# Decoder layer with attention, SSD and PEER: other instruction orders around the first gathers, part of a convolution on GpSimd, other places for late query weights

## What is computed

```python
proj = x @ w_in                      # x: 256 tokens x 1024
attn = dsa_attention(q, k, v, iq, ik, iw)   # indexer picks 64 keys for each query
ssd  = ssd_mixer(z, xbc, dt)         # depthwise conv of 4 taps, SiLU, scan in 2 chunks, gated norm
h    = LayerNorm(alpha * x + concat(attn, ssd) @ w_out)
# PEER, for each of 8 heads: scores against 2 x 128 keys, the 16 best pairs choose
# 16 of 16384 experts for each token
act  = gelu(h . u[expert]) * gate    # u, v: rows of 1024
out  = LayerNorm(alpha * h + sum over 8 x 16 experts of act * v[expert])
```

## Time and profile before

| | us |
|---|---|
| median of 3 runs | 869.95 |
| lowest, highest | 869.11, 871.92 |
| the profiled execution, its own time | 869.6 |
| its span, first to last instruction | 867.9 |
| PE, DVE, ACT, POOL busy | 574.1, 548.5, 449.4, 283.7 |

### The profile page before, as it was taken

One profiled execution on the slowest core, in us unless ns is written; L12 is line 12 of the kernel. 1 busy time (PEld: TensorE's weight loads), 2 busy tenths in 40 slices (PEclk: granted clock), 3 DMA queues, 4 the chain that ended last, 5 costly groups with the idle time before them and its releaser, 6 DMA issues.

```text
span 867.9 us, 10158 instructions
## 1 busy us (share of the span) xinstructions
PE 574.1 (66%) x3343; PEld 477.7 (55%) x3343; DVE 548.5 (63%) x1398; ACT 449.4 (52%) x804; POOL 283.7 (33%) x267
## 2 busy tenths in 40 slices
PE   7979897879576667777666554450754646555576
PEld 4458567566475666666555454350653645555532
DVE  3466556558706475656858676739968585857455
ACT  1125103645435544864867566553965665756432
POOL 0000000415224233454662544430753435344400
PEclk9979998989786789898996877865868768677689
DMA  8981003759978989999999999999999999999993
GB/s 302 386 310 50 0 1 98 266 223 399 420 268 337 407 311 392 359 404 414 421 423 420 422 420 422 420 423 422 389 421 423 423 420 422 423 422 421 422 421 132
DMA packets 58521, 301.08 MB, mean 347 GB/s; under 512 B 5576, under 2 KB 16112, under 8 KB 25712
## 3 DMA queue, kind: packets, MB, share of 16 engines
q0 software_dynamic: 36864, 268.45, 75.5%
q1 hardware_dynamic: 20400, 31.92, 10.4%
q10 hardware_dynamic: 1216, 0.19, 0.1%
HBM read 299.49 MB, written 1.05 MB: 346 GB/s over the span
## 4 chain that ended last, share of the span: by engine, by line
PE 39%; DMA 33%; DVE 13%; ACT 10%; issue 4%; POOL 1%; DVEq 0%; SPq 0%; ACTq 0%; POOLq 0%
DMA arena<-in_expert_uv,expert 29%; PE bank L620 11%; PE bank L601 7%; PE bank L470 7%; DVE arena L1439 4%; PE bank L585 3%; PE bank L482 3%; ACT arena L982 3%; PE bank L640 3%; DMA mix<-in_peer_wq 3%; ACT weight L972 2%; POOL arena L441 1%; PE bank L460 1%; DMA arena<-in_w_idx 1%; PE bank L610 1%
## 5 line engine op out<-in xcount | busy, mean ns | idle before, releaser
L620 PE MATMUL bank<-ident,arena 128*128 128x128 f32 x1920 | 307.4, 332 | 247.5 <-ACT arena L982 247.5
L441 POOL DMA_INDIRECT arena<-in_expert_uv,expert x256 | 282.0, 1102 | 542.0 <-PE bank L620 293.9
L620 PEld LDWEIGHTS bank<-ident,arena 128*128 128x128 f32 x1920 | 282.9, 175 | 271.5 <-ACT arena L982 269.3
L1439 DVE SCALAR_TENSOR_TENSOR arena<-x_sb,arena 128x1024 f32<-128x1024 f32 x256 | 304.5, 1223 | 133.2 <-DMA arena<-in_expert_uv,expert 132.7
L982 ACT ACTIVATE arena<-arena,weight 128x1024 f32<-128x1024 f32 x240 | 257.1, 1138 | 2.2
L967 ACT ACTIVATE gelu<-dots 128x4 f32<-128x4 f32 (+2 forms) x76 | 15.4, 203 | 166.8 <-DVE arena L1439 165.1
L470 PE MATMUL bank<-arena,x_t 128*128 128x512 f32 (+1 forms) x128 | 55.4, 589 | 6.2 <-DMA arena<-in_w_idx 6.2
L972 ACT ACTIVATE weight<-gelu,gate 128x1 f32<-128x1 f32 x256 | 55.9, 284 | 3.5
L601 PE MATMUL bank<-x_t,mix 128*128 128x128 f32 x384 | 45.7, 280 | 1.2 <-issue 0.8
L601 PEld LDWEIGHTS bank<-x_t,mix 128*128 128x128 f32 x384 | 45.1, 197 | 1.7 <-issue 1.0
L950 ACT ACTIVATE mix<-bank 128x256 f32<-128x256 f32 x16 | 6.1, 383 | 75.5 <-PE bank L601 75.5
(11 more groups left out here) (191 smaller groups left out, 514.4 us busy)
## 6 DMA issues: line engine op xcount, KB each, us to landing
arena<-in_w_in SPq DMA_DIRECT2D x5, 2048.0 KB, 19.8
mix<-in_peer_wq SPq DMA_DIRECT2D x6, 1024.0 KB, 9.3
arena<-in_w_out SPq DMA_DIRECT2D x2, 2048.0 KB, 17.7
arena<-in_expert_uv,expert POOLq DMA_INDIRECT x256, 22.5
arena<-in_peer_wq SPq DMA_DIRECT2D x2, 1024.0 KB, 6.9
arena<-in_w_idx SPq DMA_DIRECT2D x4, 304.0 KB, 6.8
x_t<-in_x_columns SPq DMA_DIRECT2D x4, 256.0 KB, 5.8
x_sb<-in_w_in SPq DMA_DIRECT2D x1, 1024.0 KB, 9.9
```

Of the source, the lines that this page charges most:

```text
L441: pool.indirect_dma_start(out=arena[:, slot * SLOT:(slot + 1) * SLOT], out_offset=None, in_=expert_uv, in_offset=bass.IndirectOffsetOnAxis ...
L620: last = mm(banks[2 * tile + k // 4][:, (k % 4) * P:(k % 4 + 1) * P], lhsT=arena[:, at + k * P:at + (k + 1) * P], rhs=ident[:, :], is_tran ...
L1439: ins = stt(rows, x_rows[:, bass.ds(tile * D_MODEL, D_MODEL)], 1.0, rows, ALU.mult, ALU.mult, accum_out=dots[:, parity, j:j + 1])
```

## The change

Nothing is left out of the computation. What changes:

- **Start of the token mixing.** DVE copies the transposed constants before the key projection is roped instead of after `select_keys`. PE transposes queries and keys of tile 0 ahead of the second tile's index dots, and takes `logits_of(0)` ahead of `project_xbc(0, ...)`. Tile 1's query and key transposes, `T_b` and `state` move behind `project_out(0, ...)`; `running_sums(1)` moves ahead of `logits_of(1)`; `decay_argument(1)` moves ahead of `take_logits(1)`. `qk_nat[1]` lies elsewhere for it.
- **First gathers.** `first_slots` is a new list of 80 (five units): the first two gathers use slots 10 and 11, and then 12 to 15. Slots 0, 4 and 3 join as the last three of it, so the ring has 13 slots in between. `probs_t[1]` moves from the arena to `big`.
- **Late convolution.** The three taps of tile 1 leave DVE. POOL does them with 12 `tensor_tensor` instructions of 128x512 (a product and a sum for each of three taps and two halves), put between the first unit's gathers (`LATE_TAPS`).
- **Orders in units 0 and 1.** All three engines have new orders; the gathers' sums stand between other jobs at other places; ACT's `weigh_slots` mostly stands ahead of the `take_queries` and `take_scores` of the same step; `exp_gate(2)` stands behind the first group of unit 1; the end of `take_ssd` becomes `scale_ssd`, one group later for tile 1.
- **Late queries.** Heads 4 to 7 are done one tile at a time, one for each group from group 1 of unit 2 on, instead of both tiles at four places. ACT scales a group and then copies the queries. Weights of heads 1, 2, 3 and 5, 6, 7 lie in slots 0, 4, 3, those of heads 0 and 4 in `mix`; head h + 4 is loaded when `peer_q(1, h)` is done.
- **Scores.** Units 0 and 1 get their scores straight in `side_scores`; the copy L1384 is left out in all units outside the hardware loop.
- **Banks.** PSUM banks go by the longest unused; banks 0 and 1 are taken out from `peer_q(0, 1)` on.

```diff
 def first_slots():
-    front = [12, 13, 14, 15, 4, 5]
-    return front + front + [0, 1, 2, 3] + front + [6, 7, 8, 9, 0, 1, 2, 3, 10, 11]
+    start = [10, 11, 12, 13, 14, 15, 10, 11, 1, 5, 12, 13, 14, 15, 10, 11]
+    grow = [1, 5, 12, 13, 14, 15, 10, 11, 2, 1, 5, 12, 13, 8, 9, 14]
+    ring = [6, 7, 15, 10, 11, 2, 1, 5, 12, 13, 8, 9, 14]
+    return start + grow + 2 * ring + ring[:6] + ring[6:] + ring[:6] + [0, 4, 3]
...
-    LATE_HEADS = {(2, 1): 4, (2, 3): 5, (3, 2): 6, (4, 1): 7}
+    LATE_QUERIES = {4 * 2 + 1 + n: (n % 2, 4 + n // 2) for n in range(2 * (PEER_HEADS - 4))}
...
         def head_weights(h):
-            if h in (1, 2):
-                return view(arena, (9 + h) * SLOT, KT, 2 * P)
+            if h % 4:
+                return view(arena, (0, 4, 3)[h % 4 - 1] * SLOT, KT, 2 * P)
             return view(mix, 1024, KT, 2 * P)
...
-            wait_job(sp, ("proj_xbc", 1, 0))
+            wait_job(sp, ("T_p", 1, 3))
             load_head(1)
+            wait_job(sp, ("proj_v", 1))
             load_head(2)
-            for h in range(3, PEER_HEADS):
-                wait_job(sp, ("peer_q", 1, 0 if h == 3 else h - 1))
+            wait_job(sp, ("T_y", 1))
+            load_head(3)
+            for h in range(4, PEER_HEADS):
+                wait_job(sp, ("peer_q", 1, h - 4))
                 load_head(h)
...
+                    if isinstance(u, int) and u == 0 and j in LATE_TAPS:
+                        for n, k in LATE_TAPS[j]:
+                            convolve_late(n, k)
+
+            LATE_TAPS = {1: ((0, 0), (0, 1)), 3: ((0, 2), (1, 0)), 5: ((1, 1),), 7: ((1, 2),)}
+
+            def convolve_late(n, k):
+                mine, step = xbc[:, 4 * n:4 * n + 4, P:SEQ], 6 * n + 2 * k
+                taps = conv_t[:, k * CT + 4 * n:k * CT + 4 * n + 4].unsqueeze(2).broadcast_to([P, 4, P])
+                if k == 0:
+                    pool.wait_ge(raw_ready, 2 + n + 1)
+                nc.gpsimd.tensor_tensor(tap_product, xbc_raw[:, 4 * n:4 * n + 4, P + k:SEQ + k], taps, ALU.mult).then_inc(late_tap, 1)
+                pool.wait_ge(late_tap, step + 1)
+                nc.gpsimd.tensor_tensor(mine, mine, tap_product, ALU.add).then_inc(late_tap, 1)
+                pool.wait_ge(late_tap, step + 2)
+                if k == CONV_WIDTH - 2:
+                    pool.sem_inc(conv_ready, 1)
...
# PE, units 0 and 1 after the change (sum_group(u, g) adds a pair of slots)
+            queries(0, 0)
+            scores_of_keys(0, 0)
+            project_xbc(1, 0)
+            transposed_probs(1)
+            project_xbc(1, 1)
+            project(("proj_z", 1), "z", 1)
+            sum_group(0, 0)
+            queries(0, 1)
+            sum_group(0, 1)
+            scores_of_keys(0, 1)
+            project(("proj_v", 1), "v", 1)
+            sum_group(0, 2)
+            attend(1)
...
+            sum_group(1, 4)
+            queries(1, 0)
+            sum_group(1, 5)
+            queries(1, 1)
+            scores_of_keys(1, 0)
+            sum_group(1, 6)
+            queries(1, 2)
+            scores_of_keys(1, 1)
+            sum_group(1, 7)
...
# DVE, units 0 and 1
             finish_gate(0, 0)
-            decay_argument(1)
-            convolve(1, 0)
-            convolve(1, 1)
             dot_slots(0, 0, 0, 0)
-            source_side(1)
             dot_slots(0, 0, 0, 1)
-            dot_slots(0, 0, 0, 2)
-            take_ssd(1)
-            take_attention(1)
-            dot_slots(0, 0, 0, 3)
             scores_in(0, 1)
             route_sides(1)
+            dot_slots(0, 0, 0, 2)
+            route_pairs(1)
+            dot_slots(0, 0, 0, 3)
+            take_attention(1)
+            source_side(1)
             dot_slots(0, 0, 0, 4)
-            route_pairs(1)
             finish_gate(1, 1)
+            take_ssd(1)
             dot_slots(0, 0, 0, 5)
...
+            dot_slots(0, 0, 0, 7)
+            route_pairs(0)
+            dot_slots(1, 0, 1, 0)
+            finish_gate(2, 0)
```

More of the change, by code:

```diff
@@ L70, in psum_jobs @@
-    for h in range(3, PEER_HEADS):
-        jobs += [("peer_q", 0, h), ("peer_q", 1, h), ("key_scores", 0, h), ("key_scores", 1, h)]
+    jobs += [("proj_k", 0)] + idx_dots[0] + [("proj_k", 1), ("T_qk", 0, 0), ("T_qk", 1, 0)] + idx_dots[1] + sums[0] + logits[0]
+    jobs += [("proj_xbc", 0, 0), ("proj_xbc", 0, 1)] + probs[0] + [("proj_v", 0), ("cb", 0), ("T_xs", 0), ("pv", 0), ("proj_z", 0)]
+    jobs += [("T_attn", 0), ("y_diag", 0), ("out", 0, 0), ("T_y", 0), ("out", 0, 1)]
+    jobs += [("T_qk", 0, 1), ("T_qk", 1, 1), ("T_b",)] + sums[1] + logits[1] + [("T_h", 0, 0), ("T_h", 0, 1), ("state",)]
@@ L80, in bank_plan @@
     jobs = psum_jobs()
-    sums_from = jobs.index(("T_p", 1, 0))
-    place, uses, filled = {}, {}, [0] * PSUM_BANKS
+    sums_from = jobs.index(("peer_q", 0, 1))
+    place, uses, filled, oldest = {}, {}, [0] * PSUM_BANKS, list(range(PSUM_BANKS))
     for n, job in enumerate(jobs):
-        place[job] = n % PSUM_BANKS if n < sums_from else 2 + n % (PSUM_BANKS - 2)
+        if n == sums_from:
+            oldest = [b for b in oldest if b > 1]
+        place[job] = oldest.pop(0)
+        oldest.append(place[job])
         filled[place[job]] += 1
@@ L688, in _ @@
             cb_and_xs(0)
-            transposes(("T_b",), [xbc[:, 4 + g, 0:P] for g in range(GROUPS)])
             attend(0)
@@ L692, in _ @@
             project(("proj_z", 0), "z", 0, ks=range(0, 5))
+            transposed_attention(0)
             y_diagonal(0)
+            project(("proj_z", 0), "z", 0, ks=range(5, KT))
+            project_out(0, 0, ATTN)
+            transposed_y(0)
+            project_out(0, 1, ATTN)
+            for half in range(2):
+                project_out(0, half, SSD)
+            transposed_qk(0, 1)
+            transposed_qk(1, 1)
+            transposes(("T_b",), [xbc[:, 4 + g, 0:P] for g in range(GROUPS)])
+            running_sums(1)
+            logits_of(1)
+            transposed_h(0, 0)
+            transposed_h(0, 1)
             job = ("state",)
@@ L732, in _ @@
             last.then_inc(full(job), 1)
+            sum_group(0, 3)
+            transposed_attention(1)
             y_diagonal(1)
-            for n in range(2):
-                pe.wait_ge(bank_free[n], bank_uses[n])
-            sum_group(0, 0)
-            transposed_probs(1)
-            sum_group(0, 1)
-            queries(0, 1)
-            attend(1)
-            scores_of_keys(0, 1)
-            sum_group(0, 2)
+            sum_group(0, 4)
+            queries(0, 2)
+            sum_group(0, 5)
@@ L744, in _ @@
+            scores_of_keys(0, 2)
+            project_out(1, 0, ATTN)
+            sum_group(0, 6)
+            project_out(1, 1, ATTN)
             transposed_y(1)
-            transposed_attention(1)
-            for half in range(2):
-                project_out(1, half, ATTN)
-            sum_group(0, 3)
+            sum_group(0, 7)
             project_out(1, 0, SSD)
-            sum_group(0, 4)
+            sum_group(1, 0)
             project_out(1, 1, SSD)
-            sum_group(0, 5)
-            queries(0, 2)
+            sum_group(1, 1)
@@ L1349, in add_mixed @@
                 dve.wait_ge(free(job), use(job))
-            for t in range(TILES):
-                rope_qk(0, t)
+            rope_qk(0, 0)
+            rope_qk(0, 1)
+            job = ("consts",)
+            wait_job(dve, job)
+            copy(keys_t[:, :, :], bank_view(job, 2, P))
+            copy(conv_t[:, :], bank(job)[:, 2 * P:2 * P + (CONV_WIDTH + 1) * CT]).then_inc(consts_t_ready, 1)
+            dve.wait_ge(consts_t_ready, 1)
+            dve.sem_inc(free(job), 1)
             rope_qk(1, 0)
```

272 lines of the change are left out of this document (126 added, 146 removed).

## The result

The kernel after takes 834.43 us (median of 4 runs, 832.57 to 836.31), the kernel before beside it 870.93 (4 runs, 869.11 to 876.12): ratio 0.957, 95% interval 0.952 to 0.962. The forecast was 835.0 and faster. The profiled execution took 832.65 us, its span is 830.9.

The account below looks back on a forecast made before the run. DMA-bound gathers: the end is set by their start and DMA time lost before full rate. DMA end 851 - 19.5 - 15.2 = 816.3, plus tail 16.9 and 1.7 gives 834.9, say 835 us; 8-in-10 range 818 to 853.

Parts of the forecast that it names:

- Lead: Units 0 and 1: at 221 us as many transfers landed as before at 240, 19.5 us ahead.
- loss recovered in 240 to 380 us: Units 1 to 4: of 24.2 us DMA time lost there before, 9 stay and 15.2 are gained.
- The step for the constants: Token mixing: PE's 6.15 us wait for the constants' bank goes; row sums then wait 1.9 for DVE.
- Some 5 us of slack, nothing at 1.2 each: Late convolution: POOL's taps, 14.4 us between gathers 2 to 8, cost nothing; at 2.3 each, 8 us late.
- my walk: Units 0 and 1 stepped through with the profile's durations: gathers 0 to 8 go out from 132 to 156 us.
- My bound of 10 us for PE's waits: Wrong if PE waits for a head's weights more than 10 us in sum while the DMA rate falls.
- Two of my signs: POOL's wait for PE's sums in 150 to 400 far below 93; DMA at 420 from about 225 us on.
- Rival (d): PE stops for late heads' weights, 26.3 us at all four, 17 covered; costs 37, gives 872 us; chance 0.05.
- Rival (b): Units 0 and 1: taps at 2.3 or doubled DVE stops cut the lead to 8; 846 us; chance 0.11.
- Rival (c): Nothing is lost any more: lead 22, 21.2 gained afterwards; 826 us; chance 0.12.
- (a): The ring of 13 slots starves, both stretches lose as before; 850 us; chance 0.10.
- (e): First gather starts no sooner, waiting for something else; only the order gains 12 to 15 us; 855; chance 0.03.

Follow-up runs that it names:

- The experiments with the slots and the constants: Against the changed kernel: first gathers again in slots 12 and 13, 839.72 us (0.9612); DVE's copy of the constants again behind `select_keys`, 839.44 us (0.9609).
- the control: The changed kernel itself run again, with no edit, beside the experiments made from it: 833.3 us, 0.9557 of the kernel before.
- one home: Changed kernel with weights of heads 4 to 7 all in `mix`, each asked for when the one before is read: 867.88 us, 0.9942 of the kernel before.

## Why the prediction was right, and where not

**The account** holds in its two main terms. Lead 19.5 forecast, some 18 measured; loss recovered in 240 to 380 us 15.2 forecast, 19.4 measured. The two errors, 1.5 short and 4.2 over, lie on opposite sides; with the rate of the long stretch and the tail as before that is the 830.9 of the span against my 833.2. That the forecast of 835.0 met the median of 834.43 to 0.6 us is luck: a cost of some 8 us that I had put at nothing is in it, and the other steps gave more than I had counted.

**Token mixing.** The last `project_out(0, ...)` ends at 108.9 (109.6 forecast), unit 0's experts come at 131.23 (131.9), the first gather at 132.37 (132). One term was off: the row sums wait 3.97 us for DVE and not 1.9. The timeline of PE:

```profile
54.08 3.78 PE L545 MATMUL bank<-upper,dta 128*128 128x128 f32 x16 [3.97 <-DVEq L1219]
```

The experiments with the slots and the constants agree with the reading that a microsecond of head start is a microsecond of the end: 4.6 gave 4.8, 3.8 gave 4.5. They do not prove it one for one, since each ratio is uncertain by 4 us and both profiles have a stop at head 2 besides. The step for the constants was a little large: of 6.15 I took off 1.9 for the new wait, which would leave 4.2, and the path lost 3.8 at the gather when it was undone.

**Late convolution: the step that failed.** The size was right, 1.2 us each forecast, 1.05 and 1.28 measured:

```profile
L471 POOL TENSOR_TENSOR arena<-arena,conv_t x6: 1037/1050/1062, 134.7 to 157.2; 128x512 f32<-128x512 f32 x6
```

That is the product; the sum (L473) takes 1.28. DVE's `tensor_tensor` of 128x512 (L1323) takes 0.69, so POOL takes 1.5 and 1.9 times as long. The Trainium skill, GPSIMD Engine Reference, section "When to use GPSIMD", has about twice; the traces agree for the sum and have less for the product, and on this point the rule spoke against the part with reason. But what it cost was not the size. "Some 5 us of slack, nothing at 1.2 each" was wrong: the kernel with taps on DVE is 8 us faster. I had argued that slots 12 to 15 would not be free sooner. The third gather's slot was free at 137.59 and it went out at 139.87, the fourth at 141.84 for 138.84, and the next five 5 to 10 us behind those of the kernel with taps on DVE (the ninth at 160.38 for 150.56; my walk had 156). The late issues leave DMA work undone, 4.6 us of it by 160. They also hold back the search of unit 1, since `scores_in(0, 1)` stands behind the second pair's sum on PE, which stands behind the dots of the third and fourth gather. I counted the gathers' issues and their slots but not who waits for the fourth gather's data. Two sizes came on top that my walk did not have: dots of 2.03 and 1.77 for 1.22, and a POOL sum of 2.13 for 1.28.

That the taps cost time where they stood is shown: taking them away gains 8 us, and in the profile the DMA rate of 132 to 160 us follows (301 with them, 371 without, 218 with the products doubled). By which of the two ways they cost it is not. The experiment with the taps later gave unit 1's experts back (165.53) but not the issues of the next five gathers, and it gained some 3.5 us by the ratio, none of it in its profile. It stays 4.6 us, give or take 3, behind the kernel with taps on DVE. So the moved search alone is only a part of the 8 us. What the dearer dots cost alone was not measured.

**Units 0 and 1.** The four stops of DVE were forecast as 5, 4, 5 and 4 us and are 4.88, 3.44, 4.78 and 5.13. I had priced these stops but not asked what they are worth: taking 4.88, 4.78 and 2.0 us of three of them away, in the kernel with taps on DVE, gave 7 us. Unit 1's experts came at 170.03 in the kernel after and at 167.61 in the control, where 167 was forecast; with the taps on DVE they come at 164.53.

**Units 1 to 4.** Of the reasons I gave, "`exp_gate(2)` no longer holds DVE" was worth nothing in the kernel before: there the wait could be cut by 16 us with no change of the time. What is gone from that stretch is the alternation of PE and ACT: a pair took 10.4 us, and in the kernel after the sums of three pairs of unit 1 begin at 247.11, 252.87 and 258.64, 5.8 us apart ("up to some 8" forecast). Late queries one tile at a time carry some 5 of the 19.4 us. Which of the other orders carries the rest was not taken apart.

**Loads of heads 4 to 7: right in the sign, wrong in the reason.** I had "PE waited 26 us for it and the rate stayed full". That is a misreading of the earlier trace rows: the 26.28 us are the transfer, and PE's own stop at its end was 0.44 us. So 16 slots had nothing to cover there. I also had "asked for more than 26 us ahead" and "the queue covers". The chain of the kernel after:

```profile
252.62 42.25 DMA arena<-in_peer_wq
```

These 42 us are not one load's time either. Head 5 was asked for 5 us behind head 4 and stands behind it in the same queue: head 4 landed at 273.8, head 5 at 294.9, and each further one 21 us later. A load beside gathers takes 21 us, 8.4 times a gather's 2.49, near the nine of my estimate, and up to 26 in the chains; what I left out is that four asked for close together come one after the other. PE waits for late heads 16 us in sum in 130 to 400 us:

```profile
POOL arena L455 <- PE bank L652: 108.9, 34, 8.4
...
PE bank L633 <- DMA arena<-in_peer_wq: 11.6, 3, 4.0
PE bank L633 <- DMA mix<-in_peer_wq: 4.3, 1, 4.3
```

The rate stays at 400 to 421 with the four stops at 4.3 us or less each. My bound of 10 us for PE's waits was crossed, but the rate did not fall with it. Two of my signs failed. POOL's wait for PE should have fallen far below 93.3 and is 108.9 (28 waits before, 34 now): with the queue kept full POOL waits for slots because DMA itself is the bound, so the sum of that wait says nothing; the DMA rate does. And DMA should have stood at 420 from about 225 us on; it had 400 until 280 and 411 until 340, at a full share.

**Rival (d)** is a true mechanism of this kernel, avoided by the homes. I had it as four stops of 26.3 less 17 covered, 37 in all, and gave 872. With one home it is three stops of 18, 54 us in sum, and one of 4. The control stops 11.5 us at the same three heads, so 43 us more of stops cost 33: only some 3 us of each were covered, where I had put 17, and the stops I had put at 26.3. Rival (b) held in part: the taps ate 8 us, at 1.2 us each and not at 2.3, while the stretches behind gave more than I had counted. Rival (c) was near in its second term, 21.2 against 19.4 measured, but not in its lead. Neither (a) nor (e) showed.

## What to carry to other kernels

An idle engine is a free home for work only if nothing that the bound needs queues behind that work; ask of each instruction behind it when it could start, and who waits for its data. Here the idle engine was the one that issues the gathers, and DVE, which looked busy over the whole span, was idle for three quarters of just that stretch. The small loads that were asked for beside a full queue of large ones took 21 us each, where two alone landed after 6.9, and they came one after another; so give each a place of its own, ask for it early, and count the loads ahead of it in its queue. The length of a transfer in the chain is not the stop of the engine that reads it: look at that engine's own idle time. And a long wait in the list of waits is no loss until what stands behind it is late for the bound: check the rate of the bound, not the wait.

## What the runs showed of the hardware

- POOL's two-input instructions and DVE's dots slow each other: DVE's dot of 128x1024 takes 2.03 and 1.77 us beside POOL's sums, 1.22 otherwise, and POOL's sum 2.13 for 1.28. With the taps later the dots beside them take 1.71 and 2.10 and two of the sums 2.14.
- A 1 MB load in short packets, asked for beside gathers, took 20.9 to 26.4 us in the chains of the kernel with one home, where the chain of before had 26.3.
- Four such loads in one queue landed one after another, at 273.8, 294.9, 315.9 and 336.7 us in the kernel after, 21 us apart; the 42.25 us in its chain are the second one's time from being asked for, most of the first one's included.
